# Modulation blocks placed by another table in two layers, with bias slabs, a table and an x reload at other places in the DMA queues

## What is computed

```
c_act = silu(c)
for l in range(2):
    mod = c_act @ w_ada[l] + b_ada[l]                 # 2048 x 6144 per layer
    shift, scale, gate = split(mod, 3)
    h = rmsnorm(x, norm_g[l]) * (1 + scale) + shift
    z = h @ w_in[l]                                   # 13 pieces of 512 columns
    o = mixers(z)                                     # Fourier, neighbourhood attention (needs rel_bias),
                                                      # retention, convolution; each gated by silu
    x = x + gate * (concat(o) @ w_out[l])
x = rmsnorm(x, final_g)
```

## Time and profile before

| what | value |
|---|---|
| runs before, median (lowest to highest) | 2320.24 us (2319.55 to 2324.24) |
| the profiled execution, its own time | 2315.48 us |
| its span, first to last instruction | 2313.7 us |
| PE busy | 2200.3 us, 95% of the span |
| DVE busy | 1482.2 us, 64% |
| ACT busy | 965.4 us, 42% |
| DMA moved | 509.84 MB, mean 220 GB/s |

### The profile page before, as it was taken

The page is one execution under the profiler, slowest core; times in us unless marked ns, Lnnn a source line. Parts: engine busy times, 40 slices in busy tenths (PEclk is TensorE's granted clock), DMA queues, the critical chain, the costliest instruction groups (busy, mean ns, idle before and its releaser), DMA issues.

```text
span 2313.7 us, 33056 instructions
## 1 busy us (share of the span) xinstructions
PE 2200.3 (95%) x13686; PEld 1830.5 (79%) x13686; DVE 1482.2 (64%) x1904; ACT 965.4 (42%) x1337; POOL 203.3 (9%) x388
## 2 busy tenths in 40 slices
PE   5979899998899999998999999999999999999998
PEld 3768777886697877886777787888777989988876
DVE  0445667876674677874688656576976778554554
ACT  2324544553443554554642222223436544344443
POOL 2210110111011010101001000010100010000000
PEclk8989999999999999999999999999999999999999
DMA  9988576777679767667567545563866598522253
GB/s 359 401 261 287 202 259 204 254 256 288 229 245 292 247 243 248 232 209 287 186 230 237 164 146 180 157 192 127 276 244 225 180 303 267 166 65 73 69 191 136
DMA packets 225454, 509.84 MB, mean 220 GB/s; under 512 B 36064, under 2 KB 40288, under 8 KB 222752
## 3 DMA queue, kind: packets, MB, share of 16 engines
q1 hardware_dynamic: 170048, 298.39, 38.3%
q0 software_dynamic: 55120, 209.08, 26.4%
q10 hardware_dynamic: 144, 0.36, 0.0%
...
## 4 chain that ended last, share of the span: by engine, by line
PE 72%; DMA 11%; DVE 10%; ACT 4%; issue 2%; POOL 0%; SPq 0%; DVEq 0%; ACTq 0%; POOLq 0%
PE ps L769 20%; PE ps L770 20%; PE ps L771 20%; DMA w_raw<-in_w_in 6%; DVE ada_acc L2151 3%; PE ps L825 3%; DMA ada_raw<-in_ada_w 2%; DVE wl L2238 1%; DMA w_raw<-in_w_out 1%; PE ps L1430 1%; ACT wh L1534 1%; DVE wl L2231 1%; DMA rsw<-in_ada_w 1%; PE ps L953 1%; PE ps L966 1%
## 5 line engine op out<-in xcount | busy, mean ns | idle before, releaser
L2238 DVE TENSOR_TENSOR wl<-w_raw,wh 128x1024 fp32r<-128x1024 f32 x280 | 335.3, 1223 | 267.2 <-ACT wh L1534 266.2
L1534 ACT ACTIVATE wh<-w_raw 128x1024 fp32r<-128x1024 f32 x280 | 291.7, 1056 | 439.3 <-PE ps L771 263.4
L1587 ACT ACTIVATE wh<-w_raw 128x1024 fp32r<-128x1024 f32 x220 | 230.6, 1058 | 444.2 <-PE ps L771 388.9
L769 PE MATMUL ps<-hh,wh 128*128 128x256 f32 x1280 | 375.2, 293 | 7.3 <-DVE hl L2291 7.0
L2231 DVE TENSOR_TENSOR wl<-w_raw,wh 128x1024 fp32r<-128x1024 f32 x220 | 266.5, 1221 | 179.3 <-ACT wh L1587 179.0
L770 PE MATMUL ps<-hh,wl 128*128 128x256 f32 x1280 | 364.1, 284 | 0.0
L771 PE MATMUL ps<-hl,wh 128*128 128x256 f32 x1280 | 363.4, 284 | 0.0
L2151 DVE SCALAR_TENSOR_TENSOR ada_acc<-ada_raw,cpad,ada_acc 128x1024 f32<-128x1024 f32 x264 | 330.9, 1281 | 26.0 <-DMA ada_raw<-in_ada_w 23.9
L769 PEld LDWEIGHTS ps<-hh,wh 128*128 128x128 f32 x1280 | 245.8, 192 | 31.6 <-issue 20.2
L769 PE MATMUL ps<-wh,act_hl 128*128 128x512 f32 x640 | 257.4, 402 | 6.4 <-DVE wl L2231 6.4
L770 PE MATMUL ps<-wh,act_hl 128*128 128x512 f32 x640 | 253.8, 397 | 0.0
...
## 6 DMA issues: line engine op xcount, KB each, us to landing
ada_raw<-in_ada_w POOLq DMA_DIRECT2D x272, 512.0 KB, 5.2
...
```

What stands on the lines that cost most here:

```text
L769: pe.matmul(dst, ah, bh, start=start, stop=False, skip_group_check=True)
L1534: act.activation(wh[:, g % RING, :], w_raw[:, g % RING, :], ACT.Copy).then_inc(w_hi, 1)
L1587: act.activation(wh[:, r, :], w_raw[:, r, :], ACT.Copy).then_inc(w_hi, 1)
L2238: dve.tensor_tensor(wl[:, g % RING, :], w_raw[:, g % RING, :], wh[:, g % RING, :].bitcast(F32), ALU.subtract).then_inc(w_lo, 1)
```

## The change

The change makes no instruction of arithmetic more or less. It moves five things.

1. The tables of blocks. In layer 0 the first piece of DVE ends in step 10 instead of 15, the second runs from step 11 to 20 instead of 17 to 25, the third (piece 3) from 21 to 31 instead of 26 to 33. Blocks of DVE by step, before: 1 in each of steps 0 to 15, none in 16, 1 in 17 and 18, 2 in 19 to 33. After: 1 in 0 to 7; 3, 3, 2, 1, 1, 2, 2, 1, 3 in 8 to 16; 1 in 17 and 18; 2 in 19 to 26; 1 in 27; none in 28; 1 in 29 to 31. Blocks of PE, before: 2 in steps 3 to 10, 4, 3, 3, 3, 3 in 12 to 16, 2 in 19 to 26. After: 1 in 3 to 6; 2, 2, 2, 3, 3 in 7 to 11; none in 12; 4 in each of 13 to 16; 2 in 19 to 26. In layer 1 steps 0 to 9 had DVE blocks 2, 2, 2, 2, 2, 2, 1, 1, 1, 1 and have 1, 1, 1, 1, 1, 1, 2, 2, 3, 3; PE blocks in steps 2 to 8 were 2, 2, 2, 2, 2, 3, 3 and are 1, 1, 2, 3, 3, 3, 3; in steps 26 to 31 they were 3, 3, 3, 3, 2, 2 and are 4, 4, 0, 2, 3, 3.
2. The place of the blocks inside a DVE step. In steps 8 to 25 (`ADA_AHEAD`) they come before the step's four `lo`, in steps 0 to 7 after the mixers as before, from step 26 on behind `residual`.
3. SP's queue. The bias slabs stand one behind each of slots 17 to 22 and two behind each of 23 to 27 in layer 0, and one behind each of slots 4 to 19 in layer 1. The table follows slot 17, ahead of the wait for `h_lo` that comes before the first slab.
4. POOL's queue. Since step 28 has no block, the x reload stands ahead of the first block of step 29.

5. The first group of the second block. Blocks of DVE behind the eight slots of its `u` stage, before: 0, 0, 0, 2, 2, 2, 1, 1, and the same behind the eight slots of its `gate` stage. After: 0, 0, 0, 1, 1, 1, 1, 1 and 1, 1, 1, 1, 1, 2, 2, 2. The sum stays 16.

```diff
-SLAB_AT = 5 * RING
+SLAB_SLOTS = ({**{g: 1 for g in range(17, 23)}, **{g: 2 for g in range(23, 28)}}, {g: 1 for g in range(4, 20)})
+TAB_AT = 17
...
-ADA_DVE = [{**spread(0, 0, [1] * 16), **spread(1, 17, [1, 1] + [2] * 7), **spread(3, 26, [2] * 8)},
...
+ADA_DVE = [{**spread(0, 0, [1] * 8 + [3] * 2 + [2]), **spread(1, 11, [1, 1, 2, 2, 1, 3, 1, 1, 2, 2]),
+            **spread(3, 21, [2] * 6 + [1, 0] + [1] * 3)},
...
+ADA_AHEAD = range(8, SMALL_STEP)
...
-POOL_STAGES += [s for g in range(4) for s in (("u", g, 8, 8), ("gate", g, 8, 8), ("grp", g, 2, 0))]
+POOL_STAGES += [s for g in range(4) for s in (("u", g, 8, 8 if g else (0, 0, 0, 1, 1, 1, 1, 1)),
+                                              ("gate", g, 8, 8 if g else (1, 1, 1, 1, 1, 2, 2, 2)), ("grp", g, 2, 0))]
...
-                    if g == SLAB_AT:
+                    if l == 0 and g == TAB_AT:
+                        sp.dma_start(tab[:, P:TABW], tab_d[:, P:TABW]).then_inc(tab_in, 16)
+                    if g == min(SLAB_SLOTS[l]):
                         if l:
                             sp.wait_ge(small_mul, 4 * l)
                         else:
                             sp.wait_ge(h_lo, 8)
...
+                    if g in SLAB_SLOTS[l]:
+                        first = sum(n for at_, n in SLAB_SLOTS[l].items() if at_ < g)
+                        for i in range(first, first + SLAB_SLOTS[l][g]):
+                            slab_load(l, i // 2, i % 2)
...
-                    if l == 0 and g == 20:
-                        sp.dma_start(tab[:, P:TABW], tab_d[:, P:TABW]).then_inc(tab_in, 16)
...
                 for t in range(STEPS):
+                    if t in ADA_AHEAD:
+                        ada_in_layer(t)
                     for i in range(RING):
...
                     mixers_last(t)
-                    ada_in_layer(t)
+                    if t not in ADA_AHEAD and t < SMALL_STEP:
+                        ada_in_layer(t)
...
                         if l:
                             scaled((t - OUT_STEP) // 2 - 1)
+                    if t >= SMALL_STEP:
+                        ada_in_layer(t)
```

More of the change, by code:

```diff
@@ L97, in spread @@
     return out
-ADA_DVE = [{**spread(0, 0, [1] * 16), **spread(1, 17, [1, 1] + [2] * 7), **spread(3, 26, [2] * 8)},
-           {**spread(0, 0, [2] * 6 + [1] * 4), **spread(1, 10, [1] * 14 + [2])}]
-ADA_PE = [{**spread(2, 3, [2] * 8), **spread(4, 12, [4] + [3] * 4), **spread(5, 19, [2] * 8)},
-          {**spread(2, 2, [2] * 5 + [3] * 2), **spread(3, 11, [3] * 4 + [2] * 2), **spread(4, 18, [3] * 2 + [2] * 5),
-           **spread(5, 26, [3] * 4 + [2] * 2)}]
-ADA_FIN = [{11: 2, 17: 4, 18: 0, 27: 5, 28: 1, 34: 3}, {9: 2, 10: 0, 17: 3, 25: 4, 28: 1, 32: 5}]
+ADA_DVE = [{**spread(0, 0, [1] * 8 + [3] * 2 + [2]), **spread(1, 11, [1, 1, 2, 2, 1, 3, 1, 1, 2, 2]),
+            **spread(3, 21, [2] * 6 + [1, 0] + [1] * 3)},
+           {**spread(0, 0, [1] * 6 + [2] * 2 + [3] * 2), **spread(1, 10, [1] * 14 + [2])}]
+ADA_PE = [{**spread(2, 3, [1] * 4 + [2] * 3 + [3] * 2), **spread(4, 13, [4] * 4), **spread(5, 19, [2] * 8)},
+          {**spread(2, 2, [1, 1, 2] + [3] * 4), **spread(3, 11, [3] * 4 + [2] * 2), **spread(4, 18, [3] * 2 + [2] * 5),
+           **spread(5, 26, [4, 4, 0, 2, 3, 3])}]
+ADA_FIN = [{12: 2, 17: 4, 18: 0, 27: 5, 28: 1, 34: 3}, {9: 2, 10: 0, 17: 3, 25: 4, 28: 1, 32: 5}]
 ADA_SUMMED = [(0, 1, 3), (0, 1)]
@@ L617, in _ @@
                             sp.wait_ge(h_lo, 8)
-                    if SLAB_AT <= g < SLAB_AT + HEADS:
-                        slab_load(l, g - SLAB_AT, 0)
-                        slab_load(l, g - SLAB_AT, 1)
+                    if g in SLAB_SLOTS[l]:
+                        first = sum(n for at_, n in SLAB_SLOTS[l].items() if at_ < g)
+                        for i in range(first, first + SLAB_SLOTS[l][g]):
+                            slab_load(l, i // 2, i % 2)
                     for layer, q, after in X_OUT_AT:
```

## The result

| what | before | after |
|---|---|---|
| median of the runs | 2319.39 us (2317.66 to 2324.24) | 2329.53 us (2327.97 to 2337.08) |
| ratio, with its 95% interval | | 1.0045 (1.003 to 1.0061) |
| span of the profiled execution | 2313.7 us | 2327.9 us |

A forecast was written before the change was run, and what follows sets the result against it. PE, busy for 95% of the span, was taken as the bound. Gains of 50.7 us against costs of 46.3 gave -4.4, so 2315.5 became 2311.1, plus 4.8 for the median: 2316 us, range 2304 to 2328.

The forecast's parts named there:

- (h): Layer 0 steps 13, 14, 16, layer 1 step 8: PE's last block waits for its own step's first; 14.9 us cost.
- (i): Layer 1, steps 7 and 6: PE's block waits for VectorE's of the same step; costs 3.0 and 1.2 us.
- (j): Layer 0 steps 8, 9, 10, 16, 20 to 25, layer 1 step 8: ring waits delay VectorE's `lo`; 12.1 us cost.
- (a): Layer 0, steps 5 and 6: slabs and table no longer pile up, fewer PE blocks; gain 12.3 us, at least 7.
- (c): Step 26: PE's wait for a block and the slow stretch behind it go; gain 2.5 us, at least 1.0.
- (d): Layer 0, steps 28 to 30: without blocks behind x, `lo` comes earlier; gain 5.5 us (2.5 to 8).
- (e): Layer 1, steps 4 and 6: slabs spread over 16 slots; gain 9.0 us, at least 4.3.
- (f): Layer 1, step 28: PE's blocks move to steps 26, 27 and 29 to 31; gain 3 us (0 to 7).
- (g): Second block, `u` stage: PE's four waits and the slow stretch go; gain 8.0 us, at least 4.
- the first (VectorE's lead hides its waits): Rival: VectorE catches up, so PE shows only waits behind itself and layer 1 step 7; 2297 us, chance 0.22.
- The second: Rival, layer 0 steps 8 to 10, layer 1 steps 7, 8: ring waits meet weights; 2333 us, chance 0.20.
- The third: Rival: slabs meet weights wherever they stand, PE waits in steps 4 to 6 as before; 2332 us, chance 0.12.

## Why the prediction was wrong

The costs named in (h), (i) and (j) stood where they were put, the small ones apart, but the sum of the costs was 20 us too low: the slow stretches behind the waits were mis-sized, and the wait that the moved slabs make in step 3 and the `lo` of step 13 were not counted. The list in us, predicted and measured; a gain by the length of its steps, less 0.43 for each PE block moved out, a wait as PE's idle time, a slow stretch as what is left of its step:

| term | predicted | measured |
|---|---|---|
| (a) steps 5, 6 | -12.3 | -12.3 |
| (b) step 12 | -10.4 | -10.6 |
| (c) step 26 | -2.5 | -0.8 |
| (d) steps 29, 30, 34 of layer 0 | -5.5 | -10.4 |
| (e) layer 1, steps 4, 6, without the new wait of step 6 | -9.0 | -9.0 |
| (f) layer 1, steps 26 to 31 | -3 | -1.7 |
| (g) second block | -8.0 | -6.4 |
| (h) PE behind itself | 14.9 | 15.8 |
| (i) PE behind VectorE | 4.2 | 6.4 |
| (j) VectorE ahead of `lo`, with step 13 | 12.1 | 15.6 |
| slow stretches, weights in flight | 15.1 | 22.4 |
| step 3 of layer 0 | inside (a) | +6.4 |
| all other steps | 0 | -1.2 |
| all, as a difference of the spans | -4.4 | +14.2 |

The gains came to 51.2 us, with 50.7 predicted, but in part by luck. (c), (f) and (g) gave 4.6 us less than predicted and (d) 4.9 more; and the 1.7 of (f) is what is left of 9.5 won in step 28 of layer 1 and 7.9 lost in step 30, where PE now waits 6.27 us for the `lo` behind `residual`. The prediction had neither. The costs were 46.3 predicted, and 66.6 came. Four steps failed.

1. **The slow stretch.** I took 1.7 us for each wait, from two rows of 3.4 and 2.9 us at a clock of 0.50. Behind the new waits the stretches are longer. Two of the changed kernel, both behind waits in step 13:

```profile
296.00:301.00 5.00, 5.00 (x25) 5.00 (x25) 4.84 (x7) 0.06 (x1) 0.00 (x0) 0.50 0.88 287
309.30:314.00 4.70, 4.70 (x25) 3.90 (x26) 2.13 (x2) 0.00 (x0) 1.06 (x2) 0.50 0.97 349
```

Both are at the lower level of 1.2 GHz all the time, which costs 2.5 and 2.35 us. By the length of the steps less their gaps, ten waits cost 22.4 us, 1.6 to 2.7 each, where eight times 1.7 were counted. The trace of before had longer stretches than the two that I took. These follow the waits of step 6 of layer 1 and of step 12 of layer 0:

```profile
724.10:730.90 6.80, 6.14 (x36) 4.59 (x29) 0.76 (x1) 1.85 (x2) 0.00 (x0) 0.50 0.97 267
287.00:290.60 3.60, 3.57 (x20) 2.76 (x21) 1.12 (x1) 0.00 (x0) 0.53 (x1) 0.50 0.99 382
```

In step 12 the clock was at 0.50 from 283.8 us on, so half of its 6.8 us lay in the wait and cost nothing. In step 13 after the change it fell at 294.1, 1.5 us before the wait ended, and 5.3 of 6.8 us fell on work.

2. **The moved DMAs of SP's queue.** I put the table at 2.4 us, hidden by VectorE's lead, up to 5 inside the range of (a), and gave the first slab no cost in step 3. But step 3 is 6.4 us dearer: PE waits 5.74 us there for the first block that stands behind VectorE's first. That block is a load of POOL. Tile `ada_raw`, this load from issue to landing, before (issued at 132.99) and after (issued at 134.62):

```profile
DMA to landing us min/median/max: 4.2/4.2/4.2
```

```profile
DMA to landing us min/median/max: 8.7/8.7/8.7
```

It is not the table: that was issued at 108.83 us and landed 16.2 us later, 9 us before the load was issued. SP's queue after the change:

```profile
108.83 0.47 SPq L618 DMA_DIRECT2D tab<-in_tab  x1
133.69 0.71 SPq L604 DMA_DIRECT2D slab<-in_rel  x1
134.44 0.60 SPq L615 DMA_DIRECT2D w_raw<-in_w_in  x1
```

Behind slot 17 SP now issues nothing for 24.4 us, until `h_lo` lets the first slab go. The loads of slots 18 and 19, issued at 112.48 and 116.47 before, then come together with slabs just when POOL loads its blocks. Slabs behind 17 with the table behind 20 left the load at 8.8 us; slabs and table behind 20 brought it back to 4.2 and step 3 down by 7.8 us, but steps 5 and 6 took 10.7 more. So the slabs' place makes this wait, and from step 3 to 6 the wait goes where they go. In layer 1 slabs alone, with no table, were enough. How much in layer 0 is due to the slabs' own rows, and how much to the weights that the `h_lo` wait holds back, no run separates. The cover that I named was that of the wrong queue.

3. **Step 13's `lo`.** (j) counted only waits on the ring. In step 13 nothing waits for the ring on VectorE, and PE still waits 3.19 us, since the convolution taps, two blocks and the `lo` add up to 3.1 + 2.6 + 1.2 us from 288.65 on, and PE is there at 292.4. With the slow stretch this is 5.7 us.

4. **Small terms of (i) and (j).** Step 6 of layer 1 waited 3.0 and not 1.2 us: the load took 5.7 us with weights in flight (issued 730.7, landed 736.4). Step 16's `wl` 3.8 and not 3.0, step 8's 3.7 and not 3. In the sum for step 9, 225.86 less 216.72 is 9.1 and not 9.0.

(d) went the other way, 10.4 for 5.5. The 5.5 is PE's wait for the late `lo` alone: the slow stretch behind it goes as well (step 30 is 7.6 us shorter), and so does the `ptr` wait of step 29 (1.6 us, with its stretch 2.3); the run with all old tables shows 8.3 us from the place on VectorE alone.

Of the rivals, the first (VectorE's lead hides its waits) fell: in steps 8, 9, 13 and 16 waits for `wl` of 3.2 to 3.8 us reached PE. The second had the right sign, but in layer 0 the self-gated loads of steps 9 to 16 landed after 3.9 to 4.4 us, not 7.4, as the load issued at 304.81 (used at 309.25) shows, and so did that of step 7 of layer 1 (4.1). It held in step 8 of layer 0, where the third block's load took 7.5 us, and in part in step 6 of layer 1 (5.7). The estimate of 3.2 us from the figures of the Trainium skill ("DMA: Bandwidth & Descriptors", "Anatomy of one DMA — SWDGE (gpsimd) path") is below all of these. The third fell for the changed kernel as a whole, but is half true for the queue part alone, which is worth 4 us and not 21.
